# Two DRAM-to-DRAM window copies of a decoder step: issued by SyncE between weight blocks instead of by GpSimd

## The reference, cut to what matters

```python
    wk = jnp.concatenate([ck_win, kw], axis=1)     # ck_win: (8, 512, 2, 64) float32
    wv = jnp.concatenate([cv_win, vw], axis=1)
    ...
    return o.reshape(n, ds, D_Q), wk[:, -wb:], wv[:, -wb:]      # wb = 512
```

## Time and profile before

| | |
|---|---|
| median of 3 runs | 1747.99 us (1747.68 to 1752.9) |
| profiled execution, its own time | 1750.72 us |
| its span in the trace | 1749.1 us |
| TensorE busy | 1678.5 us, 96% of the span |
| VectorE, ScalarE, GpSimd busy | 1138.0, 887.1, 220.2 us |
| granted TensorE clock, mean | 0.983 of full speed |

### The profile page before, as it was taken

One profiled execution on the slowest core, in us unless ns is written; L12 is line 12 of the kernel. 1 busy time (PEld: TensorE's weight loads), 2 busy tenths in 40 slices (PEclk: granted clock), 3 DMA queues, 4 the chain that ended last, 5 costly groups with the idle time before them and its releaser, 6 DMA issues.

```text
span 1749.1 us, 27553 instructions
## 1 busy us (share of the span) xinstructions
PE 1678.5 (96%) x10018; PEld 1303.8 (75%) x10018; DVE 1138.0 (65%) x1550; ACT 887.1 (51%) x1006; POOL 220.2 (13%) x262
## 2 busy tenths in 40 slices
PE   7999999999998999999999999999999999999998
PEld 4899978788777678767768675867768585876765
DVE  6766785655446757948477593938567493838661
ACT  5245655533323336737365573728465473727461
POOL 0022010003312123101000101000100100100100
PEclk9999999999999999999999999999999999999999
DMA  5064234214328318999999999999999999999995
GB/s 225 23 217 123 73 113 82 73 62 133 118 58 307 117 55 325 357 392 411 392 404 375 401 402 403 380 396 408 381 406 392 397 400 399 398 392 409 389 399 219
DMA packets 103715, 498.76 MB, mean 285 GB/s; under 512 B 20658, under 2 KB 37146, under 8 KB 53056
## 3 DMA queue, kind: packets, MB, share of 16 engines
q1 hardware_dynamic: 82512, 454.20, 66.0%
q0 software_dynamic: 20976, 42.93, 9.1%
q10 hardware_dynamic: 144, 0.55, 0.1%
HBM read 488.10 MB, written 25.35 MB: 294 GB/s over the span
## 4 chain that ended last, share of the span: by engine, by line
PE 78%; DMA 10%; DVE 6%; issue 3%; ACT 3%; SPq 0%; POOL 0%; ACTq 0%; DVEq 0%; POOLq 0%
PE bank L1274 24%; PE bank L1292 13%; DMA ring<-in_w_exp 9%; PE bank L757 7%; PE bank L657 5%; PE bank L812 5%; PE bank L1343 4%; PE bank L1328 3%; PE bank L684 3%; PE bank L1077 2%; PE bank L825 1%; DMA slab<-in_w_tok 1%; PE bank L846 1%; PE bank L1245 1%; PE bank L1249 1%
## 5 line engine op out<-in xcount | busy, mean ns | idle before, releaser
L2516 DVE TENSOR_TENSOR ring_rounded<-ring,wide_rounded 128x2048 fp32r<-128x2048 f32 x126 | 283.7, 2286 | 22.0 <-ACT wide_rounded L1751 21.9
L1751 ACT ACTIVATE wide_rounded<-ring 128x2048 fp32r<-128x2048 f32 x126 | 236.8, 1912 | 71.0 <-DMA ring<-in_w_exp 51.7
L1274 PE MATMUL bank<-ring_rounded,slab_rounded 128*128 128x512 f32 x672 | 262.4, 391 | 0.0
L1274 PE MATMUL bank<-xn_rounded,slab_rounded 128*128 128x512 f32 x672 | 221.7, 401 | 0.0
L2516 DVE TENSOR_TENSOR ring_rounded<-ring,xn_rounded 128x2048 fp32r<-128x2048 f32 x84 | 189.7, 2286 | 48.6 <-ACT xn_rounded L1751 48.1
L1751 ACT ACTIVATE xn_rounded<-ring 128x2048 fp32r<-128x2048 f32 x84 | 159.5, 1910 | 77.1 <-DMA ring<-in_w_exp 76.3
L1292 PE MATMUL bank<-wide_rounded,slab_rounded 128*128 128x512 f32 x504 | 170.5, 399 | 1.3 <-DVE slab_rounded L2610 1.3
L2656 DVE TENSOR_SCALAR slab<-bank 128x256 f32<-128x256 f32 x22 | 9.3, 425 | 238.0 <-PE bank L1328 238.0
L1274 PE MATMUL bank<-wide_rounded,slab_rounded 128*128 128x512 f32 x504 | 159.0, 390 | 0.0
L1328 PE MATMUL bank<-ring,slab 128*64 128x256 f32 x1408 | 156.2, 380 | 0.0
L757 PE MATMUL bank<-ring_rounded 128*128 128x260 f32 x768 | 149.6, 294 | 2.3 <-DVE slab_rounded L2124 2.3
(11 more groups left out here) (536 smaller groups left out, 3019.7 us busy)
## 6 DMA issues: line engine op xcount, KB each, us to landing
ring<-in_w_exp SPq DMA_DIRECT2D x384, 1024.0 KB, 12.8
ring<-in_w_blk SPq DMA_DIRECT2D x40, 512.0 KB, 3.8
slab<-in_w_tok SPq DMA_DIRECT2D x4, 1304.0 KB, 15.2
ring<-in_w SPq DMA_DIRECT2D x8, 512.0 KB, 3.3
ring<-in_w_out SPq DMA_DIRECT2D x2, 2048.0 KB, 16.0
xn<-in_xT SPq DMA_DIRECT2D x4, 520.0 KB, 7.9
ring<-in_k_cmp SPq DMA_DIRECT2D x32, 64.0 KB, 3.7
ring<-in_k_cmp POOLq DMA_DIRECT2D x32, 64.0 KB, 2.8
```

Of the source, the lines that this page charges most:

```text
L1274: r = mm(bank[:, c, :], a[:, 4 * h + k, :], w[:, k, :], start=False, stop=h == 1 and k == 3 and x == 2)
L1751: fn(WH[(2 * c + h) % 6], ring[:, half_of(c, h)], ACT.Copy).then_inc(S["wh_ready"], 1)
L2516: v.tensor_tensor(ring_r[:, half_of(c, h)], ring[:, half_of(c, h)], WHf[(2 * c + h) % 6], ALU.subtract)\
```

## The change

SyncE issues the two copies inside its loop over the weight blocks: the key copy right behind block 25, the value copy right behind block 29, both with no wait of their own. They signal a new semaphore `window_out`, for which SyncE waits at the end. GpSimd issues neither any more. Besides, the last of four VectorE copies into `hrep` now counts on `smp_dve`, where before an own instruction signalled `hrep_ready`; TensorE waits for one semaphore there instead of two, and later counts on `smp_dve` are one higher.

```diff
@@ sync
                 block(j)
+                if j == 25:
+                    sp.dma_start(d["o_kwin"][:, :, 0:WIN - 1], d["k_win"][:, :, 1:WIN]).then_inc(S["window_out"], 16)
+                if j == 29:
+                    runs = "n (a b) c -> a n (b c)"
+                    sp.dma_start(d["o_vwin"][:, 0:WIN - 1, :].rearrange(runs, b=7), d["v_win"][:, 1:WIN, :].rearrange(runs, b=7))\
+                        .then_inc(S["window_out"], 16)
             for b in range(4):
                 hidden_weights(0, b)
...
-            sp.wait_ge(S["outs_done"], 16 * 6)
+            sp.wait_ge(S["outs_done"], 16 * 4)
+            sp.wait_ge(S["window_out"], 16 * 2)
@@ tensor
             compressed_values(0)
-            pe.wait_ge(S["hrep_ready"], 1)
-            pe.wait_ge(S["smp_dve"], 3)
+            pe.wait_ge(S["smp_dve"], 4)
@@ vector
-                    mine(v.tensor_copy(hrep[:, f, h, :, :], src))
+                    mine(v.tensor_copy(hrep[:, f, h, :, :], src), S["smp_dve"] if f and h else None)
             mine.settle()
-            dve.sem_inc(S["hrep_ready"], 1)
@@ gpsimd
             dma(d["o_sconv"], xps).then_inc(S["outs_done"], 16)
-            dma(d["o_kwin"][:, :, 0:WIN - 1], d["k_win"][:, :, 1:WIN]).then_inc(S["outs_done"], 16)
-            runs = "n (a b) c -> a n (b c)"
-            dma(d["o_vwin"][:, 0:WIN - 1, :].rearrange(runs, b=7), d["v_win"][:, 1:WIN, :].rearrange(runs, b=7)).then_inc(S["outs_done"], 16)
             pool.wait_ge(S["kv_out"], 16 * (TT + 1))
```

More of the change, by code:

```diff
@@ L365, in build @@
             k_pages_in k_pages_in_pool v_pages_in v_pages_in_pool w2_in
-            xs_hi xs_lo xp_hi xp_lo cs_done p1_copied gh_raw xp_ready vt_done cp_done pp_copied ghp_raw gh_gelu hrep_ready ck_done ck_copied ck_act
+            xs_hi xs_lo xp_hi xp_lo cs_done p1_copied gh_raw xp_ready vt_done cp_done pp_copied ghp_raw gh_gelu ck_done ck_copied ck_act
             att_s att_max att_p att_w att_pc att_ce att_cs att_ta att_pa att_pv att_o vwin_in
@@ L374, in build @@
             wh_ready wl_ready y_scaled y_added
-            outs_done""".split()}
+            outs_done window_out""".split()}
         x_rows_in, t_out = ([sem(f"{n}{b}") for b in (0, 1)] for n in ("x_rows_in", "t_out"))
@@ L1030, in _ @@
             for first, b, tiles, vals, turned in ((2, 1, 4, vwin, ptw), (6, 0, NPG, vslc, pts)):
-                pe.wait_ge(S["smp_dve"], 5 - b)
+                pe.wait_ge(S["smp_dve"], 6 - b)
                 if b:
@@ L1057, in _ @@
             pe.wait_ge(S["att_o"], 2 * QT_N)
-            pe.wait_ge(S["smp_dve"], 6)
+            pe.wait_ge(S["smp_dve"], 7)
             for m in range(3):
                 pb_half(m, 0)
-            pe.wait_ge(S["smp_dve"], 7)
+            pe.wait_ge(S["smp_dve"], 8)
             pe.transpose(bank[0:HD, 1, 0:NROW], oS[R, :], ident[R, R]).then_inc(S["smp_pe"], 1)
             pb_half(3, 0)
-            pe.wait_ge(S["smp_dve"], 8)
+            pe.wait_ge(S["smp_dve"], 9)
             for m in range(KD):
@@ L2754, in _ @@
             second_pages("vslc", d["v_slc"], S["v_pages_in_pool"])
-            pool.wait_ge(S["smp_dve"], 8)
+            pool.wait_ge(S["smp_dve"], 9)
             dma(bias_raw, d["b_up"]).then_inc(S["bup_in"], 16)
```

## The result

| | before | after |
|---|---|---|
| median of 4 runs each | 1749.79 us (1747.68 to 1752.9) | 1809.89 us (1808.38 to 1811.19) |
| profiled execution, its span | 1749.1 us | 1809.1 us |
| mean granted clock | 0.983 | 0.969 |

The change makes the kernel slower: the ratio is 1.0346, 95% interval 1.033 to 1.0362. The forecast was 1807 us in a range of 1797 to 1832. The kernel before has one run more here than the three whose median the forecast started from, 1747.99 us.

The account below looks back on a forecast made before the run. The prediction took TensorE, busy 96% of the span, to bound the kernel. Its terms, +61.0 - 3.5 + 1.5 = +59.0 us on 1747.99, gave 1807 us, range 1797 to 1832.

Parts of the forecast that it names:

- The value copy's engine: Value copy behind block 29 on SyncE: expected on one DMA engine at 26.4 GB/s, 79.3 us long.
- What queues behind it: SyncE's queue: one of block 30's sixteen shares stands behind the value copy, so block 30 lands at 358.3 us.
- The stall: TensorE at `values`, line 846, waits for ScalarE's attention copy, held up by block 30: +61.0 us.
- GpSimd's side: GpSimd no longer issues the value copy: VectorE's 2.0 us hold of TensorE and 1.5 us low clock go, -3.5 us.
- The clock: TensorE after the long stall: lower clock level charged at +1.5 us, +3 if it lasts twice as long.
- three large terms: The stall at +61.0 us, GpSimd's issue gone at -3.5 us, the clock after the stall at +1.5 us.
- A: Rival: value copy is spread when SyncE issues it, block 30 lands before it is wanted; 1744.5 us, 7%.
- B: Rival: value copy on one engine, but block 30 passes beside it in SyncE's queue; 1744.5 us, 4%.
- C: Rival: value copy much slower from SyncE, runs handled singly or SyncE held; at half rate 1886 us, 6%.
- The parts taken at nothing: Key copy behind block 25, at most a few us late, and `hrep` signal, between 0 and 1.0 us: each taken as 0.

## Why the prediction was right

**The value copy's engine.** Taken: one engine at 26.4 GB/s, from GpSimd's row. Measured in SyncE's queue: 1.02 engines, 26.2 GB/s. The kernels with 16 and 146 at the front show that the front dimension makes it so. By the rule cited in the prediction from the Trainium skill (DMA: Bandwidth & Descriptors, "Why a DMA increments its semaphore by 16 and not by 1") the counts for 73, 146 and 16 are 1, 2 and 16; the runs show 1.02, 2.1 and 13.5 on average over 6 us. Only these three fronts were run.

**What queues behind it.** Taken from `w2`'s landing. Block 30 was to land 82.4 us behind the copy's issue (358.3 - 275.86); it landed 281.35 + 75.2 - 272.26 = 84.3 us behind it. The kernel with the copy in ScalarE's queue shows that it is the queue. One thing on the way was not as forecast: block 31 was to be issued some 10 us behind block 30, but SyncE was held (see the last section) and issued it at 337.8. It landed 20.0 us later, at 357.8, as forecast right behind block 30, so this cost nothing here.

**The stall.** 61.0 us forecast, 62.2 measured; the 1.9 us by which the block is later are partly made good by ScalarE's two instructions.

**GpSimd's side.** -3.5 us forecast. SyncE issues the value copy at 272.26, where before that place was 275.86: 3.6 us earlier. The kernel with 16 at the front gives it as 0.18% (3.1 us). Only the 2.0 us of TensorE's wait are tied to the hold on VectorE. The other 1.5 us were a low clock in the profiled execution of the kernel before; in the kernel with the `hrep` signal alone the same wait had no low clock behind it. That this part came out at its full size in this pair of profiles is partly luck.

**The clock.** +1.5 us forecast, with up to 3 named for a long pause. In windows of the changed kernel:

```profile
300.00:350.00 50.00, 0.00 (x0) 0.00 (x0) 0.00 (x0) 0.00 (x0) 0.00 (x0) 0.50 0.13 46
...
358.40:364.00 5.60, 5.60 (x28) 4.19 (x28) 4.00 (x10) 2.00 (x6) 0.00 (x0) 0.50 0.00 0
364.00:370.00 6.00, 6.00 (x53) 5.15 (x53) 3.36 (x9) 3.16 (x7) 0.00 (x0) 1.00 0.26 89
```

TensorE works from 358.4 to 364.0 at 0.50, the level of 1.2 GHz, after 62 us of nothing: 5.6 us at half speed cost 2.8 us. That is 1.3 us more than the term, in proportion the largest error of the three.

**The sum.** 62.2 - 3.6 + 2.8 = 61.4 us; the measured medians differ by 60.1 and the spans by 60.0. The missing 1.3 to 1.4 us come from the clock at two other places. Up to 535 us of the kernel before, the changed kernel's TensorE runs 61.4 us behind it, 17 us further on only 58.5 (before, after, before, after):

```profile
535.75 1.09 PE L970 MATMUL bank<-ident,xn 128*128 128x128 f32 x8
597.12 1.09 PE L977 MATMUL bank<-ident,xn 128*128 128x128 f32 x8
...
552.62 1.04 PE L1018 MATMUL bank<-xn,kT 128*64 128x128 f32 x8
611.14 1.04 PE L1024 MATMUL bank<-xn,kT 128*64 128x128 f32 x8
```

In between, the kernel before ran at a granted clock of 0.52 and the changed one at 1.00:

```profile
545.00:552.00 7.00, 7.00 (x62) 6.88 (x64) 2.49 (x7) 0.87 (x3) 0.00 (x0) 0.52 1.12 393
...
606.40:613.40 7.00, 6.28 (x92) 5.83 (x90) 4.78 (x13) 0.76 (x3) 0.00 (x0) 1.00 1.15 382
```

Near the end it is the other way round: from 1678.8 to 1683.7 us of the kernel before the distance grows from 58.7 to 60.1, with a clock of 0.76 before (1678 to 1685 us) and of 0.51 after (1736 to 1743). In all, 61.4 - 2.9 + 1.6 = 60.1. Of the low stretch at 545 us too the runs show no fixed cause: the kernel with the key copy alone has one there, the one with the `hrep` signal alone has none.

So the mechanism was right and the closeness of the number was partly luck. The forecast of the difference was 59.0. Its three large terms were 2.4 us too small together, and 1.4 us of clock elsewhere hid part of that. The forecast of the time, 1807 against 1809.89, is a further 1.8 us low, because the median that it started from was 1747.99 and that of four runs is 1749.79.

**The rivals.** A (the copy is spread) does not happen in the change, but the kernel with 16 at the front is exactly it: 1747.7 us, a ratio of 0.9982 against the 0.998 that the sum of -3.5 gives. B (beside) happens across queues only. C (half the rate) does not happen: the copy moved 26.2 GB/s. But one of the reasons that were given for it, a SyncE that is itself held, is seen, as the last section shows. The parts taken at nothing, the key copy and `hrep`, cost nothing in their own runs.

## What to carry to other kernels

Before a DMA is moved into a queue that carries loads in time, look at the largest divisor up to 16 of its outermost dimension: 511 rows cut as 73 x 7 ran on one engine, the same bytes cut as 16 x 4088 per sequence on about all. That the divisor sets the number rests here on three fronts, 73, 146 and 16. A transfer with a strange time to landing is harmless only as long as nobody queues behind it; the load behind it in the old trace (94.3 us for 384 KB) gave the price of the move before it was made. And a gain and a trap can sit in one edit: with the pattern mended the move wins 0.2%, mending the pattern by itself 0.1%, and moving the copy to ScalarE's queue 0.3%. The intervals of the three overlap, so these runs do not rank them.

## What the runs showed of the hardware that was not expected

SyncE itself was held, which the prediction named only in a rival. The issue of block 30 took 56.42 us, where an issue of a block takes 0.33; with 146 at the front it took 26466 ns:

```profile
L528 SPq DMA_DIRECT2D ring<-in_w_blk x1: 26466/26466/26466, 281.1 to 281.1; - x1
```

The block's other fifteen shares did not run before the release either. In the window 336 to 358 us of the changed kernel (GB/s in 40 slices of 0.55 us) they come at about 338, the next block's at about 345. One engine goes on alone, with the copy until 355 and with its shares of the two blocks until 357.5:

```profile
GB/s 33 26 26 26 145 264 369 220 26 26 26 26 26 26 26 26 71 220 294 354 86 26 26 26 26 26 26 26 26 26 26 26 26 33 21 30 22 30 22 0
```

So the copy delayed the block twice, first by holding SyncE until 337.8 and then, for the share on its own engine, until 356.5. The second alone decides the time here, since it ends last; the first would decide it for anything that SyncE has to issue in between, on whatever engines it runs.

A queue with room for a limited number of pieces per engine fits both kernels. At the release, 17.2 us of the copy were left in the changed kernel (337.8 to 355.0), 126 of its 584 pieces at 137 ns. With 146 at the front the release came at 307.6 and the copy ended at 316.4, 8.8 us later, which was 123 of the 584 pieces of each engine. The time that was left differs by half, the number of pieces hardly. Such a limit is an inference and was not tested. It does not account for all: block 31's issue was held for another 6.8 us, until 344.6, when only 76 pieces of the copy and block 30's share were still ahead of it.
